# Gate matrices read back for 16 blocks at a time instead of 8, in other buffers

## What is computed

```
def peer(h, w_pq, sub_keys, u_exp, v_exp):          # 16,384 experts, 8 heads, 16 picks each
    q = (xb @ w_pq).reshape(TOK_BLOCK, PEER_HEADS, 2, D_KEY_HALF)
    s = einsum('thcd,hcnd->thcn', q, sub_keys)
    ...                                              # top 16 of both halves, top 16 of their sums
    g = softmax(top_s)
    a = gelu(einsum('thkd,td->thk', u_exp[eidx], xb))
    return einsum('thk,thkd->td', g * a, v_exp[eidx])
```

## Time and profile before

| | |
|---|---|
| median of 3 runs | 3987.83 us (3984.5 to 3989.89) |
| profiled execution, own time | 3981.41 us |
| its span in the trace | 3979.6 us |
| mean granted clock of TensorE | 0.987 |
| u products, layer 0 and 1 | about 598 to 1384 us, 2493 to 3279 us |
| v products, layer 0 and 1 | about 1384 to 2051 us, 3279 to 3948 us |
| DMA | 244 GB/s over the span |

### The profile page before, as it was taken

How to read it: one execution, slowest core, us unless ns; L and a number is a source line. 1 busy time by engine, 2 the same in 40 slices (tenths; PEclk the granted TensorE clock), 3 DMA queues, 4 the chain that set the end, 5 groups by cost and what they waited for, 6 DMA issues and landing times.

```text
span 3979.6 us, 57585 instructions
## 1 busy us (share of the span) xinstructions
PE 3838.0 (96%) x21170; PEld 3355.6 (84%) x21170; DVE 2916.1 (73%) x4499; ACT 1673.6 (42%) x2920; POOL 2279.5 (57%) x1240
## 2 busy tenths in 40 slices
PE   7978899999999999999989989999999999999998
PEld 5756898888888888888879989888888888888886
DVE  4775218899875499999983320889987549999997
ACT  3265323556666422223231131355666643222322
POOL 1101224666666688888842222467666668888884
PEclk8999999999999999999999999999999999999999
DMA  5302324788888899999954312378888889999995
GB/s 209 129 2 81 127 85 138 264 281 305 302 302 308 313 342 317 330 319 327 335 181 175 117 54 90 131 257 285 300 302 300 311 314 341 314 327 322 321 333 185
DMA packets 396808, 972.44 MB, mean 244 GB/s; under 512 B 32160, under 2 KB 221344, under 8 KB 382880
## 3 DMA queue, kind: packets, MB, share of 16 engines
q1 hardware_dynamic: 301664, 630.72, 46.9%
q0 software_dynamic: 92160, 335.59, 22.7%
q10 hardware_dynamic: 2752, 3.21, 0.2%
HBM read 835.37 MB, written 133.96 MB: 244 GB/s over the span
## 4 chain that ended last, share of the span: by engine, by line
PE 57%; issue 26%; POOL 12%; DVE 4%; DMA 1%; DVEq 1%; ACT 0%; POOLq 0%; ACTq 0%
PE PS L775 30%; PE PS L763 18%; PE PS L565 5%; POOL SL L445 5%; POOL ROWS L452 4%; POOL SL L436 3%; PE PS L755 3%; DVE ROWS L1262 1%; PE PS L716 1%; DVE OH L1251 1%; DMA ROWS<-u_exp,EI 1%; DVE PO L1188 0%; DVE TS L1183 0%; DVE ABF L1218 0%; PE PS L548 0%
## 5 line engine op out<-in xcount | busy, mean ns | idle before, releaser
L445 POOL TENSOR_TENSOR SL<-RW,SH 128x1024 fp32r<-128x1024 f32 x512 | 1333.2, 2604 | 728.6 <-ACT SH L989 715.4
L989 ACT CAST SH<-RW 128x1024 fp32r<-128x1024 f32 x512 | 537.2, 1049 | 1430.3 <-PE PS L775 826.5
L763 PE MATMUL PS<-HH,SH 128*128 128x480 f32 x2048 | 799.6, 390 | 5.5 <-POOL SL L445 4.2
L775 PE MATMUL PS<-WH,SH 128*128 128x480 f32 x2048 | 777.0, 379 | 2.2 <-ACT GE L995 1.3
L763 PE MATMUL PS<-HH,SL 128*128 128x480 f32 x2048 | 776.5, 379 | 0.0
L763 PE MATMUL PS<-HL,SH 128*128 128x480 f32 x2048 | 776.3, 379 | 0.0
L775 PE MATMUL PS<-WH,SL 128*128 128x480 f32 x2048 | 775.2, 379 | 0.0
L775 PE MATMUL PS<-WL,SH 128*128 128x480 f32 x2048 | 775.1, 378 | 0.0
L436 POOL TENSOR_TENSOR SL<-RW,SH 128x1024 fp32r<-128x1024 f32 x84 | 202.6, 2416 | 808.3 <-ACT SH L820 808.3
L1312 DVE TENSOR_TENSOR WL<-GL,WH 128x480 fp32r<-128x480 f32 x256 | 558.6, 2182 | 20.6 <-ACT WH L1028 17.4
L1251 DVE TENSOR_TENSOR OH<-PS,PK 128x1024 f32<-128x1024 f32 x240 | 291.5, 1220 | 221.7 <-PE PS L755 207.7
(11 more groups left out here) (171 smaller groups left out, 5225.5 us busy)
## 6 DMA issues: line engine op xcount, KB each, us to landing
RW<-u_blk SPq DMA_DIRECT2D x256, 512.0 KB, 4.5
RW<-v_blk SPq DMA_DIRECT2D x256, 512.0 KB, 5.9
gate_acts<-GE SPq DMA_DIRECT2D x256, 240.0 KB, 3.2
router_weights<-GT SPq DMA_DIRECT2D x60, 1024.0 KB, 5.0
GB<-router_weights SPq DMA_DIRECT2D x32, 1920.0 KB, 14.5
GL<-gate_acts SPq DMA_DIRECT2D x256, 240.0 KB, 5.5
RW<-wstream SPq DMA_DIRECT2D x100, 512.0 KB, 4.3
AW<-wpairs SPq DMA_DIRECT2D x40, 1024.0 KB, 4.9
```

Of the source, the lines that this page charges most:

```text
L445: nc.gpsimd.tensor_tensor(SL[:, r % 2], RW[:, r % RAW], SH[:, r % 2].bitcast(F32), ALU.subtract).then_inc(raw_used, 1)
L763: last = mm(PS[:, n % 2, NG:NS], w[:, n % 2, j], a[:, j, NG:NS], start=(j == 0 and q == 0), stop=(j == DJ - 1 and q == 2))
L775: last = mm(PS[:, dj, NG:NS], w[:, k % 2, dj], a[:, k, NG:NS], start=start, stop=stop)
L989: nc.scalar.copy(SH[:, r % 2], RW[:, r % RAW]).then_inc(hi_done, 1)
```

## The change

A group is 16 blocks instead of 8, so a GB buffer has 30 x 16 x 16 floats per partition, 30,720 bytes instead of 15,360. There are 8 loads per layer instead of 16. The first buffer moves from BIG (behind the gathered rows) to the place of X, which is 20,480 bytes long, and on into the first 10,240 bytes of H, where the one-hot tiles were; the second stays at HH and grows into HL. The conditions of issue are rewritten for the new size, and X's return to its place, still at step 112 (NB_E - GROUP), has a wait of its own ahead of it, since the group of blocks 96 to 111 lies there.

```
-GROUP = 8
+GROUP = 16
...
-    GB = [sb(f"GB{k}", [P, NTG, GROUP, TG], F32, at=at)[0] for k, at in enumerate((at_BIG + 16384, at_HH))]
+    GB = [sb(f"GB{k}", [P, NTG, GROUP, TG], F32, at=at)[0] for k, at in enumerate((at_X, at_HH))]
...
-                if n % GROUP == GROUP - 1 and n + 9 < NB_E:
-                    load_gates((n + 9) // GROUP)
-                if n == NB_E - 16:
+                if n % GROUP == GROUP - 1 and n + GROUP + 1 < NB_E:
+                    load_gates((n + GROUP + 1) // GROUP)
+                if n == NB_E - GROUP:
+                    sp.wait_ge(w_done, (l + 1) * NB_E - GROUP)
                     sp.dma_start(X[:], x_dram).then_inc(x_back, 16)
```

## The result

The changed kernel takes **4036.7 us** (median of 3 runs, 4032.2 to 4039.2) where the kernel before takes 3987.8: ratio 1.0122, 95% interval 1.0099 to 1.0145. The forecast was 4034 us. The profiled execution took 4039.2 us, with a span of 4037.4, so it stands 2.5 us over the median, while that of the kernel before (3981.4) stands 6.4 under its own. Between the two profiles lie 57.8 us, between the medians 48.9. Sums over the traces are made against the 57.8.

The account below looks back on a forecast made before the run. TensorE was taken as the bound, with DMA and VectorE right behind. Mid-stream loads 17, block 1's load 7, first load 14 and clock 8 make 46 us, forecast on the median 3987.8 as 4034 us, range 3993 to 4082.

Parts of the forecast that it names:

- TensorE has nothing to gain, RW decides: Expert products: TensorE busy 3838 of 3979.6 us; loss comes if weights RW land late behind the larger GB load.
- Price of a 1 KB packet: GB loads: 49.6 ns per 1024-byte packet against 29.5 at 512 bytes, so each load lasts 7.1 us longer.
- The bound by which twice the bytes cost twice the time: GB loads: upper bound of 59 ns per 1 KB packet, each load lasting 10.4 us longer.
- RW after 19.0 us: Behind mid-stream GB loads: RW lands 19.0 us after issue, 11.9 + 7.1, past the limit by 1.4.
- The limit of 17.6: v products: time from RW's issue to landing beyond which TensorE stands, 17.6 us.
- The three waiting terms: TensorE waits: +17 us behind twelve mid-stream loads, +7 behind those of v block 1, +14 behind the first loads.
- the mid-stream term: Six GB loads per layer in mid-stream: RW 1.4 us past the limit, twelve times, +17 us (0 to 56).
- The clock: After the first load's gap of about 8 us, TensorE's clock falls: 4 us per layer, +8 us (0 to 10).
- Rival 1: GB loads: 1 KB packets cost 59 ns, each load lasts 10.4 us longer; 4087 us, chance 0.08.
- Rival 2: Mid-stream: late GL makes VectorE the bound, TensorE pays about 4.5 us per load; 4071 us, chance 0.17.
- Rival 3: Behind GB loads: growth under 5.7 us is hidden from RW; 3994 us, or 4000 with the clock, chance 0.15.
- Rival 4: DMA engines: fewer loads save 18 us per layer and shorten other transfers; about 3984 us, chance 0.03.

Follow-up runs that it names:

- mid_split: Changed kernel with the six mid-stream GB loads per layer each issued in two halves, 8 steps apart: 4014.8 us, ratio 1.0072 to the kernel before.
- gb_act: Changed kernel with the six mid-stream GB loads per layer issued on ScalarE's queue, same size: 4009.9 us, ratio 1.0069 to the kernel before.
- all_split: As mid_split, with the two first GB loads per layer split too, so nothing over 1920 KB goes out: 3984.9 us, ratio 1.0001 to the kernel before.
- places: Changed kernel with groups of 8 again, buffers in the new places, X back at step 120: 3986 us, ratio 0.9997 to the kernel before.
- pieces512: Changed kernel with each GB load as two back-to-back transfers of 8 blocks in 512-byte pieces, same bytes: 4089.4 us, ratio 1.0263 to the kernel before.
- mid_26_4: As mid_split, but in parts of 26 and 4 token groups instead of 15 and 15: 4013.9 us, ratio 1.0075 to the kernel before.
- u_split: Changed kernel with only each layer's first GB load split, blocks 0 to 7 and 8 to 15: 4019.8 us, ratio 1.0086 to the kernel before.

## Why the prediction was right

The sum was 17 + 7 + 14 + 8 = 46 us, and 48.9 came. Step by step:

- **TensorE has nothing to gain, RW decides.** Right: mid_split, gb_act and all_split take the loss away by RW alone, places shows that nothing else of the change costs.
- **Price of a 1 KB packet**, 49.6 ns from a line between two sizes: 48.6 and 48.8. The bound by which twice the bytes cost twice the time was not met (59 ns). The rule of the Trainium skill behind that bound (DMA: Bandwidth & Descriptors, Specifications) is not borne out here: pieces512, all in 512-byte pieces, takes 1.4% longer than the change for the same bytes.
- **Landing and limit.** RW after 19.0 us: 18.9 behind the first mid-stream load, 19.3 in the mean of the twelve. The limit of 17.6, read off a single late cast behind X's return, held: 16.8 us still costs nothing (mid_26_4), nor do 17.5 and 17.6, and behind the loads with 17.9 and more TensorE stood.
- **Idle time.** The three waiting terms, 17 + 7 + 14 = 38 us, are 37.9 in the trace: 16.6 behind the twelve mid-stream loads, 7.7 behind those of block 1, and 15.6 instead of 1.6 behind the first ones. For the mid-stream term this is so near by luck. It was 1.4 us twelve times; in the trace a load costs between nothing and 4.1 us, and two loads make up half. Their 4 us come from a gate load that itself went out late behind VectorE, a path that the sum did not have.
- **The clock is the term that was mis-sized**, at 8 us for 17.0 in the profile, and in its places too. I had a fall of the clock behind the first load only, at 8 us; there it cost 4.0, since much of the fall passed while TensorE had nothing to do (in layer 0 it was busy for about 3.0 us of 6.8). The v products, where I had nothing, lost 13.0: behind the load of block 1 in both layers and behind three of the twelve mid-stream loads, two of them the ones of 4 us. I had looked only at whether a gap of 8 us throttles, and not asked it of the gaps of 4 us that my own sum put behind the load of block 1. With the first load split, the v products idle for 28.2 us instead of 25.8 (u_split), so part of its wait only moves on.
- **Against the profile's own time the sum was low**: 46 for 57.8, and 9.0 of the 11.8 are the clock. Against the medians it was near, since one profiled execution was on the fast side and the other on the slow one. The interval of the ratio reaches from 39 to 58 us, so the medians cannot tell the two sums apart.
- **Rival 1** had 4087 us for two packets' worth of time per kilobyte, and pieces512, which is that, takes 4089. The parts differ: by the profile the v products of both layers are 82 us longer than before and the u products 22, where the rival had 70 and 29.
- **Rival 2** was half there. Its sign, ScalarE's cast of w waiting for VectorE block after block, came in 129 of 256 blocks, 365.0 us for 93.6, and by the forecast's own words that was a sign of being wrong. In two of the twelve loads the late VectorE did make the gate load and the RW behind it late, 4 us of idleness each. But it did not do so every time, and TensorE did not pay 4.5 us per load but 1.4 in the mean. How much the late casts of w add elsewhere no run isolates. **Rival 3** failed on the growth of the load: RW landed 7.0 us later (18.9 for 11.9), not less than 5.7. **Rival 4**: fewer packets did free DMA time, and nobody waited for it (all_split, ratio 1.0001).

## What to carry to other kernels

A prefetch has a deadline, and the largest transfer ahead of it in its queue decides whether it is met, not the mean load of the engines: compare (landing behind the burst) with (issue to first use) for the stream that the bottleneck engine consumes. Merging loads saves packets but lengthens the burst; when the total is hidden anyway, only the second counts, and splitting the load in time or giving it another queue takes the cost away. A gap of a few us on TensorE should be priced with the fall of its clock, and of that fall only the part in which TensorE has work.

## What the runs showed that I had not expected

- **A small stream on a queue of its own can cost more than it saves.** GL is 240 KB per block. When it was moved to a third queue, the weights came later during the burst, 22.2 us for 18.9, and the kernel was 28 us slower. That its share of the engines is the reason is argued, not isolated.
- **Who is held by a large load is who issues next on its queue.** SyncE's next RW took 9.40 us to issue behind a 3840 KB load; with the load on ScalarE's queue, which issues nothing behind it, SyncE's took 0.33 us.
- **All of the mid-stream loss hangs on the last eighth of a load.** 3328 KB ahead of RW cost nothing in mid-stream, 3840 KB cost 20 us.
- **The same load between the same neighbours does not always cost the same.** Twelve like ones cost from nothing to 4.1 us of idleness. The two dearest are those where the GL load ahead of them in SyncE's list had waited longest for VectorE, 5.3 us.
